# Seven block products for most up-projection tiles of two layers, with the weights' sums on GpSimd

## What is computed

```python
D_MODEL = 1024; SEQ = 256; DEPTH = 2; D_FF = 2816; FFN_CONV = 3
...
def causal_dwconv(x, w):
    k_w = w.shape[0]
    s = x.shape[1]
    xp = jnp.pad(x, ((0, 0), (k_w - 1, 0), (0, 0)))
    return sum(xp[:, j:j + s, :] * w[j] for j in range(k_w))
...
    x = layer_norm(DEEPNORM_ALPHA * x + mix, ln1_g, ln1_b)
    hid = causal_dwconv(x @ w_up, ffn_conv_w) + ffn_conv_b
    gate, val = jnp.split(hid, 2, -1)
    ffn = (jax.nn.silu(gate) * val) @ w_down
    return layer_norm(DEEPNORM_ALPHA * x + ffn, ln2_g, ln2_b)
```

## Time and profile before

| | |
|---|---|
| median of three runs | 2255.62 us (2252.44 to 2256.43) |
| the profiled execution | 2251.84 us, of which the span of the core is 2250.0 us |
| PE busy in the span | 1784.6 us, 79% |
| DVE, ACT, POOL busy | 552.9, 308.8 and 32.7 us |
| up part of layer 0, from its first matmul to its last | 192.5 to 346.5 us |
| down part of layer 0 | 346.5 to 413.5 us |
| up part of layer 1 | 592.5 to 746.5 us |
| experts | about 975 us to the end |

### The profile page before, as it was taken

One profiled execution on the slowest core, in us unless ns is written; L12 is line 12 of the kernel. 1 busy time (PEld: TensorE's weight loads), 2 busy tenths in 40 slices (PEclk: granted clock), 3 DMA queues, 4 the chain that ended last, 5 costly groups with the idle time before them and its releaser, 6 DMA issues.

```text
span 2250.0 us, 29462 instructions
## 1 busy us (share of the span) xinstructions
PE 1784.6 (79%) x12314; PEld 971.0 (43%) x12314; DVE 552.9 (25%) x1290; ACT 308.8 (14%) x742; POOL 32.7 (1%) x42
## 2 busy tenths in 40 slices
PE   8999999999999999987666666666665665666665
PEld 7867885786788566432211221221121121122122
DVE  3444338444433744420100101010010010010101
ACT  3231110223211112310000000000000000000001
POOL 0010000001100000000000000000000000000000
PEclk9999999999999999988867777877777777887877
DMA  8234552623544365399999999999999999999998
GB/s 289 76 113 142 191 177 108 221 103 113 159 151 150 131 224 210 131 397 415 424 424 425 424 425 424 425 424 425 425 425 425 425 424 425 425 425 424 425 425 342
DMA packets 150153, 693.86 MB, mean 308 GB/s; under 512 B 15936, under 2 KB 65664, under 8 KB 96962
## 3 DMA queue, kind: packets, MB, share of 16 engines
q1 hardware_dynamic: 143922, 683.68, 75.5%
q0 software_dynamic: 6016, 9.04, 1.2%
q10 hardware_dynamic: 144, 0.13, 0.0%
HBM read 691.72 MB, written 4.22 MB: 309 GB/s over the span
## 4 chain that ended last, share of the span: by engine, by line
PE 54%; DMA 37%; SPq 4%; DVE 2%; issue 2%; ACT 1%; DVEq 0%; ACTq 0%
DMA arena<-in_w_up 35%; PE bank L608 16%; PE bank L1210 7%; PE bank L634 6%; PE bank L761 6%; PE bank L1229 5%; SPq L415 3%; PE bank L1059 1%; PE bank L756 1%; PE bank L968 1%; DVE arena L2052 1%; PE bank L1063 1%; PE bank L988 1%; DMA arena<-in_w_down 1%; PE bank L694 1%
## 5 line engine op out<-in xcount | busy, mean ns | idle before, releaser
L1210 PE MATMUL bank<-arena 128*32 128x512 f32 (+1 forms) x3072 | 467.3, 764 | 282.7 <-DMA arena<-in_w_up 250.4
L608 PE MATMUL bank<-arena 128*128 128x256 f32 (+1 forms) x2208 | 381.9, 335 | 4.0 <-DMA arena<-in_w_in 2.7
L1210 PEld LDWEIGHTS bank<-arena 128*32 128x32 f32 x3072 | 112.0, 137 | 627.9 <-DMA arena<-in_w_up 333.9
L608 PEld LDWEIGHTS bank<-arena 128*128 128x128 f32 x2208 | 345.7, 191 | 41.4 <-issue 3.9
L1229 PE MATMUL bank<-arena 128*32 128x256 f32 x2816 | 229.3, 478 | 113.3 <-DMA arena<-in_w_down 104.3
L2052 DVE TENSOR_TENSOR arena<-arena,bank 64x256 f32<-64x256 f32 x96 | 40.1, 418 | 707.4 <-ACT arena L1496 705.7
L1229 PEld LDWEIGHTS bank<-arena 128*32 128x32 f32 x2816 | 97.3, 134 | 241.0 <-DMA arena<-in_w_down 131.7
L761 PE MATMUL bank<-arena 128*128 128x256 f32 x576 | 138.6, 387 | 0.0
L634 PE MATMUL bank<-arena 128*128 128x512 f32 x308 | 132.7, 592 | 0.0
L1496 ACT ACTIVATE arena<-bank 64x512 f32<-64x512 f32 (+1 forms) x48 | 23.2, 549 | 749.6 <-PE bank L1210 749.6
L1886 DVE SCALAR_TENSOR_TENSOR arena<-bank,arena 128x254 f32<-128x254 f32 (+1 forms) x176 | 76.8, 478 | 184.3 <-ACT arena L1423 181.0
(11 more groups left out here) (295 smaller groups left out, 1324.9 us busy)
## 6 DMA issues: line engine op xcount, KB each, us to landing
arena<-in_w_gate SPq DMA_DIRECT2D x127, 1408.0 KB, 20.3
arena<-in_w_up SPq DMA_DIRECT2D x127, 1408.0 KB, 23.3
arena<-in_w_down SPq DMA_DIRECT2D x144, 1024.0 KB, 17.6
arena<-in_w_down SPq DMA_DIRECT2D x32, 1536.0 KB, 13.4
arena<-in_w_up SPq DMA_DIRECT2D x44, 1024.0 KB, 7.7
arena<-in_w_in SPq DMA_DIRECT2D x40, 1024.0 KB, 8.6
arena<-in_w_out SPq DMA_DIRECT2D x12, 1024.0 KB, 6.0
arena<-in_w_down SPq DMA_DIRECT2D x12, 512.0 KB, 4.2
```

What stands on the lines that cost most here:

```text
L608: last = mm(ps[bank][:, j * S + lo:j * S + lo + n], w[:, k, c:c + P], xT[:, k, lo:lo + n], start=(k == 0), stop=(k == KT - 1))
L1210: last = mm(ps[b][32 * q:32 * q + 32, 0:n], expert_x[:, k, :], w, start=(k == 0), stop=(k == KT - 1))
```

## The change

The tiles 3 to 21 of both layers are computed by block products. A tile's product has the two rows of weight blocks (the gate channels and the value channels of the tile), the two halves of the 1024 input channels, and the two halves of the tokens. Eight products of such quarters, each four matmuls deep, become seven. Tiles 0 to 2 remain as they are.

- **PE** (`up_block_products`, new): 7 x 4 = 28 matmuls of 128 columns for a tile in place of 16 of 256 columns. The seven products lie in seven quarters of a pair of banks: (2, 3) for tile 3, then (4, 5) and (0, 1) in turn. It waits for `up_sums` before the fourth product of seven and reads the summed weights, and it may begin tile j when `up_summed` has counted tile j - 2.
- **GpSimd** (`up_sums`, new): for each such tile four additions or subtractions over 512 columns (128 partitions by 4 blocks of 128), two operands in SBUF and the result in SBUF, with a `drain` after the first, the third and the fourth. Three results go to a ring of three buffers (`UP_RING`) in memory that the attention of the layer used before; the fourth replaces a part of the weights in their slot. It starts when the output product of the layer has ended. In layer 0 the four copies in DRAM are issued between tiles; in layer 1 the sums follow the twelve transfers.
- **DVE**: once a layer four sums of `xT` over 512 columns. For each tile `up_summed`: a copy of 128 columns from PSUM and five additions or subtractions of an operand in SBUF and one in PSUM (two of 256 columns and three of 128), which leave the four quarters of the result in `up_blocks` in SBUF. Of the taps both tensor operands now lie in SBUF. The order is `up_summed(j)`, product of hidden values j - 1, taps j. The sums of down pairs 0 and 1 follow tiles 17 and 19 rather than 19 and 20.
- **ACT**: the silu of tile j - 1 comes ahead of the last tap of tile j from tile 4 on, and the last tap reads `up_blocks`.
- The down part's first products wait for `up_summed` of the last two tiles in place of `up_convolved`; some semaphores are merged, and buffers lie at other places.

```diff
-UP_BANKS = (0, 1, 4, 5)
+UP_BANKS = (0, 1, 4)
+PAIR_BANKS = {0: (4, 5), 1: (0, 1)}
+FIRST_PAIR_BANKS = (2, 3)
+UP_RING = 3
+UP_PLACE = {1: (0, 0), 2: (0, 1), 6: (0, 2), 5: (0, 3), 3: (1, 0), 7: (1, 1), 4: (1, 2)}
...
+            def up_sums(l, j):
...
+                pool.wait_ge(sem(f"slot_in{r}"), l * (UNITS // RING * 32 - first) + 32 * (u // RING + 1) - first)
+                if j >= AHEAD + UP_RING:
+                    pool.wait_ge(sem("up_product"), at(l, "up_product", j - UP_RING + 1))
...
+                nc.gpsimd.tensor_tensor(s1, w[:, 0:4, cg], w[:, 4:8, cg], ALU.add)
+                pool.drain()
+                nc.gpsimd.tensor_tensor(s2, s1, w[:, 0:4, cv], ALU.subtract)
+                nc.gpsimd.tensor_tensor(w[:, 0:4, cg], w[:, 0:4, cv], w[:, 0:4, cg], ALU.subtract)
+                pool.drain()
+                nc.gpsimd.tensor_tensor(s4, w[:, 4:8, cv], s2, ALU.subtract)
+                pool.drain().then_inc(sem("up_sums"), 1)
...
-                    for n in range(4):
-                        pool.wait_ge(sem("up_product"), 4 + 3 * n)
...
+                    pool.wait_ge(sem("rows_used"), ROW_UNITS + 1)
+                    for j in range(AHEAD, FT):
+                        if j in (6, 9, 12, 15):
...
+                        up_sums(l, j)
...
+            for j in range(AHEAD, FT):
+                up_sums(DEPTH - 1, j)
...
-                        pe.wait_ge(sem("up_convolved"), at(l, "up_convolved", FT - 2))
+                        pe.wait_ge(sem("up_summed"), at(l, "up_summed", FT - AHEAD - 1))
...
-                        pe.wait_ge(sem("up_convolved"), at(l, "up_convolved", FT))
+                        pe.wait_ge(sem("up_summed"), at(l, "up_summed", FT - AHEAD))
...
+                    for m in (1, 2, 4, 5, 6, 7, 3):
+                        if m == 5:
+                            pe.wait_ge(sem("up_sums"), at(l, "up_sums", j - AHEAD + 1))
+                        left, right = left_right[m]
+                        b, at_ = UP_PLACE[m]
+                        for k in range(4):
+                            last = mm(ps[pair[b]][:, at_ * P:(at_ + 1) * P], left[:, k, :], right[:, k, :], start=(k == 0), stop=(k == 3))
...
-                    if j >= 4:
-                        pe.wait_ge(sem("up_convolved"), at(l, "up_convolved", j - 3))
-                    up(j).then_inc(sem("up_product"), 1)
+                    if AHEAD < j <= AHEAD + 2:
+                        pe.wait_ge(sem("up_convolved"), at(l, "up_convolved", AHEAD if j == AHEAD + 1 else 2))
+                    elif j > AHEAD + 2:
+                        pe.wait_ge(sem("up_summed"), at(l, "up_summed", j - 2 - AHEAD + 1))
+                    up_block_products(j).then_inc(sem("up_product"), 1)
...
+                    v.wait_ge(sem("up_product"), at(l, "up_product", j + 1))
+                    w.tensor_copy(up_blocks[:, 6:7, :], block(pair, 1))
+                    v.drain()
+                    w.tensor_tensor(up_blocks[:, 0:5:4, :], up_blocks[:, 6:7, :].broadcast_to([P, 2, P]), block(pair, 2, 2), ALU.add)
+                    v.drain()
+                    w.tensor_tensor(up_blocks[:, 5:6, :], up_blocks[:, 4:5, :], block(pair, 5), ALU.add)
+                    w.tensor_tensor(up_blocks[:, 6:7, :], up_blocks[:, 4:5, :], block(pair, 7), ALU.add)
+                    v.drain()
+                    w.tensor_tensor(up_blocks[:, 1:4:2, :], up_blocks[:, 5:6, :].broadcast_to([P, 2, P]), block(pair, 3, 2), ALU.add)
+                    w.tensor_tensor(up_blocks[:, 2:3, :], up_blocks[:, 6:7, :], block(pair, 4), ALU.subtract).then_inc(sem("up_summed"), 1)
...
-                    if j in (19, 20):
-                        v.drain()
-                        down_sums(j - 19)
+                    if j in (17, 19):
+                        v.drain()
+                        down_sums((j - 17) // 2)
```

More of the change, by code:

```diff
@@ L497, in _ @@
             pool.dma_start(const[:, 2 * P + 4:NC], a["consts"][:, 2 * P + 4:NC]).then_inc(sem("const_in"), 16)
+            def up_sums(l, j):
+                u = U_UP + j // 2
+                r, first = u % RING, 16 if u % RING == 0 else 0
+                pool.wait_ge(sem(f"slot_in{r}"), l * (UNITS // RING * 32 - first) + 32 * (u // RING + 1) - first)
+                if j >= AHEAD + UP_RING:
+                    pool.wait_ge(sem("up_product"), at(l, "up_product", j - UP_RING + 1))
+                w = slot(u, 512)
+                cv, cg = (slice(c, c + P) for c in (j % 2 * P, j % 2 * P + 2 * P))
+                s1, s2, s4 = (up_weight_sums[j % UP_RING][:, n] for n in range(3))
+                nc.gpsimd.tensor_tensor(s1, w[:, 0:4, cg], w[:, 4:8, cg], ALU.add)
[5 more added lines that the diff above has]
+                pool.drain().then_inc(sem("up_sums"), 1)
             pool.wait_ge(sem("bias_copied"), 1)
@@ L1001, in _, with up, up_block_products @@
                 last.then_inc(sem("rows_used"), 1)
-                def up(j, t=None):
-                    return channels(U_UP + j // 2, j % 2, UP_BANKS[j % 4], t=t, step=2)
+                def up(j, t):
+                    return channels(U_UP + j // 2, j % 2, UP_BANKS[j], t=t, step=2)
+                def up_block_products(j):
+                    w = slot(U_UP + j // 2, 512)
+                    cv, cg = (slice(c, c + P) for c in (j % 2 * P, j % 2 * P + 2 * P))
+                    s1, s2, s4 = (up_weight_sums[j % UP_RING][:, n] for n in range(3))
+                    t1, t2, t3, t4 = (x_sums[:, n] for n in range(4))
+                    left_right = {
+                        1: (w[:, 0:4, cv], xT[:, 0:4, 0:P]),
+                        2: (w[:, 4:8, cv], xT[:, 4:8, 0:P]),
+                        3: (s4, xT[:, 4:8, P:S]),
+                        4: (w[:, 4:8, cg], t4),
+                        5: (s1, t1),
+                        6: (s2, t2),
+                        7: (w[:, 0:4, cg], t3),
+                    }
+                    pair = FIRST_PAIR_BANKS if j == AHEAD else PAIR_BANKS[j % 2]
+                    for m in (1, 2, 4, 5, 6, 7, 3):
[5 more added lines that the diff above has]
+                            last = mm(ps[pair[b]][:, at_ * P:(at_ + 1) * P], left[:, k, :], right[:, k, :], start=(k == 0), stop=(k == 3))
+                    return last
                 pe.wait_ge(sem("x0_copied"), at(l, "x0_copied", 2))
@@ new lines, in _ @@
+                t1, t2, t3, t4 = (x_sums[:, n] for n in range(4))
+                (b11, b12), (b21, b22) = ((xT[:, k:k + 4, 0:P], xT[:, k:k + 4, P:S]) for k in (0, 4))
+                v.drain()
+                v.wait_ge(sem("x1_copied"), at(l, "x1_copied", 4))
+                w.tensor_sub(t1, b12, b11)
+                w.tensor_sub(t3, b22, b12)
+                v.drain()
+                w.tensor_sub(t2, b22, t1)
+                v.drain()
+                w.tensor_sub(t4, t2, b21).then_inc(sem("x1_copied"), 1)
@@ new lines, in hidden_product @@
+                def hidden_product(j):
+                    v.wait_ge(sem("gate_silu"), at(l, "gate_silu", j + 1))
+                    w.tensor_mul(hidT[:, j, :], ff_conv[:, j % 3, 0, :], ff_conv[:, j % 3, 1, :]).then_inc(sem("hidden_ready"), 1)
+                for j in range(FT):
+                    if j >= AHEAD:
+                        up_summed(j)
+                    if j > AHEAD:
+                        hidden_product(j - 1)
+                    v.wait_ge(sem("up_last_tap"), at(l, "up_last_tap", j + 1))
+                    for s in range(1, FTAPS):
+                        for gv in range(2):
+                            c = (2 - s) * 2 * FT + gv * FT + j
+                            from_ = ps[UP_BANKS[j]][:, gv * S:(gv + 1) * S - s] if j < AHEAD else up_blocks[:, 2 * gv:2 * gv + 2, :].rearrange("p x y -> p (x y)")[:, 0:S - s]
+                            last = w.scalar_tensor_tensor(ff_conv[:, j % 3, gv, s:S], from_, conv_w[:, 48 + c:49 + c], ff_conv[:, j % 3, gv, s:S], ALU.mult, ALU.add)
+                        if s < FTAPS - 1:
+                            v.drain()
+                    last.then_inc(sem("up_convolved"), 1)
+                    v.drain()
+                    if 0 < j <= AHEAD:
+                        hidden_product(j - 1)
+                    if j in (17, 19):
+                        v.drain()
+                        down_sums((j - 17) // 2)
@@ L1898, in _ @@
+                hidden_product(FT - 1)
                 v.drain()
```

88 lines of the change are left out of this document (46 added, 42 removed).

## The result

The changed kernel takes 2317.48 us, the median of six runs (2315.38 to 2320.21); the kernel before takes 2254.66 us, the median of six (2252.44 to 2256.43). The ratio is 1.0283, with an interval of 1.0273 to 1.0293. The forecast was 2231 us, the range 2228 to 2284: the change makes the kernel slower, and by more than the range allowed.

What follows compares the result with a forecast made beforehand. PE was taken to bound the up parts: 13.0 us gained less 0.8 us at the joint to the down part is 12.2 us a layer, 24.4 in both, so 2231 us by the median; range 2228 to 2284 us.

Steps and rivals of the forecast that it cites:

- PE's part: Up parts: 28 matmuls take 6.25 us a tile, 0.68 us less; 13.0 us a layer, 26.0 us in both.
- The wait at the joint: Start of the down part: its first products wait for up_summed of the last two tiles, 0.5 to 1 us.
- Rival 3: Up parts: short accumulations cost 0.235 us a matmul, 6.6 us a tile, 12 of 26 us go: 2243 us; chance 0.05.
- POOL's duration: Up parts: POOL's four sums and three drains take 6.0 us a tile, between 5.4 and 7.0 us.
- Rival 2: Up parts: POOL alone too slow, 7.1 us a tile gives 2240 us, 7.5 us a tile 2253; chance 0.12.
- this margin: Up part: about 9 us that POOL may lose over 16 tiles at no cost, up to 6.8 us a tile.
- rival 1: Up parts: DVE's two-SBUF-operand instructions and POOL's take turns; 2266 to 2292 us, chance 0.29; mild form 2238 to 2252, 0.13.
- A: From the experiments, layer 0: a POOL drain after POOL's own transfer lasts until that has landed, 12 to 16 us, four times.
- B: From the experiments, both layers: DVE instructions with two SBUF operands take turns with POOL's sums; taps 4.91 us, alone 1.83.

Runs made afterwards that it cites:

- the best kernel: Against the changed kernel: layer 0's copies last, result blocks in PSUM, down sums after tiles 18 and 21, POOL's first sums after the layer norm; 2234.81 us.

## Why the prediction was wrong

**PE's part was right.** 6.25 us a tile, PE busy without a break and 141 us for the part were forecast, and the kernel without the sums and the best kernel show them (141.8 us in the best). 12.2 us a layer and 24.4 in all were forecast; the spans of 2250.0 and 2231.8 us differ by 18.2, the medians by 21.8, and the two layers by 11.0 and 11.7 in the table. The wait at the joint, taken at 0.8 us, was 0.6 and 0.9 in the kernel without the sums. Without POOL's sums beside it DVE needs what was forecast, too: where it has fallen behind and POOL stands still, its tiles are 5.12 us apart (260.07 to 265.19 in the changed kernel), forecast 5.1. Rival 3 (short accumulations) is out: 93.81 us for 840 records.

**POOL's duration was right, by luck.** A tile's sums with nothing outstanding take 5.6 to 5.8 us from one tile to the next; forecast 6.0, range 5.4 to 7.0. But the four sums take 1.27 us each where 1.1 was taken, and the three drains leave gaps of 0.14 to 0.24 us where 0.53 was taken, so two errors cancelled. Rival 2, POOL alone too slow, is false as it was put, and yet POOL became the bound of layer 0, for a reason that it did not name.

**The first step that failed: "In layer 0 the four copies (1.18 us each, 4.7 us in all) come out of this margin."** The margin was 9 us. What they took was 4.5 us of issuing and 57 us of gaps at the drains behind them. 1.18 us is the time of issuing, and that is all that the earlier trace rows could show, since before no drain stood behind a copy: the only POOL gaps at drains there, 0.49 to 0.64 us, had no transfer outstanding. I priced the drain by those rows and never asked what else it waits for. The copy's time to land can be read in the view of the transfers of the kernel before:

```profile
bias_rows<-bias_rows POOLq DMA_DIRECT2D x4, 768.0 KB, 15.8
```

It would have given the size of the price, as an estimate: four times 15.8 us less the margin of 9 us, some 54 us of stall on POOL. This alone makes the changed kernel slower by 46 us (2298.6 against 2252.4 for the kernel before on that chip), with the gain of the seven products already taken off.

**The second: "The taps and the product stay at 1.82 and 0.43 us if operands in SBUF cost what those in PSUM do."** Where POOL is quiet they do (481 ns a tap without the sums). Beside POOL's sums the taps took 3.8 to 5.4 us and the product up to 1.5, and DVE's tile, taken at 5.1 us, became longer than PE's 6.25. This is rival 1, which was given 0.29 and not the forecast's place. Its mechanism, its place (taps and product), its sign and its bound hold. It foresaw +5 to +18 us a layer against before; layer 1 shows +13.0, layer 0 with the copies last +11.0. The tile took 7.1 and 8.0 us in turn, 7.6 in the mean, and up to 8.7 us in the first half of layer 1's part, where it said 6.8 to 7.5. Its account of who waits was off, though: 1.5 to 2 POOL instructions in the way, 1.7 to 2.4 us on DVE, were expected; the taps lost 2.0 to 3.6 us and the product up to 1.0, while of POOL's four sums one or two lost 0.2 to 0.3 us each. The reason that I gave against it, 4.59 us of idle time on DVE, was weak, since the same text had already spent that time. "No row shows such a wait" was no evidence either, for no row had both kinds of instruction at once. What the prediction cites on exactly this pair of instructions from the Trainium skill ("SBUF — State Buffer", Who interferes with whom), with rows that agree with its other half, was better evidence than an absence; the runs agree with it, with 4.91 us for the taps beside POOL's sums when both operands lie in SBUF and 1.82 when one lies in PSUM.

**What the two together did.** The price of A hid that of B in layer 0, and B alone worked in layer 1. The long waits cost more than their own time as well: PE's granted clock falls in them and is still low when PE starts again. In windows of the changed kernel:

```profile
222.50:237.40 14.90, 14.90 (x134) 14.72 (x132) 9.83 (x29) 3.88 (x9) 2.46 (x2) 1.00 0.67 201
237.40:257.00 19.60, 11.80 (x82) 11.79 (x82) 6.67 (x13) 2.06 (x5) 13.89 (x11) 0.74 0.30 103
```

The second begins with PE's wait of 7.80 us, and its mean clock is 0.74. Cut finer, the clock is 0.96 from 237.4 to 241.0 and 0.50, which is 1.2 GHz, from 241.0 to 251.0; PE works again from 245.2 on, so 6 us of its work run at half the clock. From 251.0 on it is 1.00. The block products of layer 0 are busy 131.6 us rather than 119.0, those of layer 1 125.4. So layer 0 is 47.8 of waits + 12.6 of clock - 12 of gain = 48.4 us slower, measured 49.0 (192.9 to 462.9 against 192.5 to 413.5); layer 1 18.8 + 6.4 - 11.7 = 13.5, measured 13.0.

**The range.** Its upper end took in most of rival 1 and nothing of a stall of POOL behind a transfer. Of the marks that I named, rival 1's (taps long though ACT has finished, PE waiting at a tile's start for `up_summed`) and rival 2's (PE waiting in the middle of a tile for POOL, POOL never idle) were both there; the second with the difference that POOL stood still. Rival 1's third mark, POOL's instructions well over 1.2 us, was hardly there: most stayed at 1.27 us.

## What to carry to other kernels

Before arithmetic moves to an engine that also issues transfers, ask of each `drain` on it what is outstanding at that moment: the price is the rest of the transfer's time to land, not the gap that a quiet drain shows; put transfers last, or wait on the semaphore of the instruction whose result is needed. Before GpSimd gets a steady load of SBUF reads, count the VectorE instructions beside it that have two SBUF operands, and give each an operand in PSUM where a bank is free. And when no row of a profile shows two things at once, price their meeting as a case of its own; that no row shows a wait is no evidence against it.

## What the runs showed that I had not expected

- POOL stood still for 12.1 to 16.2 us at a `drain` behind its own transfer in DRAM (768 KB, 14.4 to 18.5 us to land), until 0.1 to 0.2 us after the landing; a wait for the semaphore of the same sum, with the same transfer under way, left 0.08 us.
- The turn-taking falls unevenly. DVE's taps of 255 columns, 0.46 us each, became 0.95 to 1.35 us beside POOL's 512 columns, while these mostly stayed at 1.27 to 1.28 us, with 1.43 to 1.58 for one or two of the four in a tile beside the taps. Against DVE instructions of 1024 columns POOL lost too: 2.07 and 2.04 us rather than 1.28, and DVE 1.93 rather than 1.28.
- PE's granted clock fell in waits of 8 to 12 us: 0.62 to 0.75 as the mean of the four stretches of 15 to 20 us around one. In layer 1 it stayed at 1.00 from 706 to 730 and from 738 to 760 us, with waits of 0.4 to 1.7 us, and was 0.61 in the 4 us after the wait of 5.53 us.
